# One level of Strassen's method in the up projection of a decoder step's MLP on one core

## What is computed

```python
def merge_and_mlp(x, o, pool_out, w_out, g_mlp, w_up, w_down):
    B, T, _ = x.shape
    mix = jnp.concatenate([o.reshape(B, T, ATTN_WIDTH).astype(x.dtype),
                           pool_out.astype(x.dtype)], axis=-1)
    h = x + mix @ w_out
    a = jnp.square(jax.nn.relu(rms_norm(h, g_mlp) @ w_up))
    return h + a @ w_down
```

## Time and profile before

| | |
|---|---|
| median of the runs | 899.13 us (897.83 to 900.75, 3 runs) |
| the profiled execution | 892.73 us, of which the trace spans 890.9 us |
| PE busy in the span | 819.0 us, 92% |
| DVE, ACT, POOL busy | 429.2 us, 345.5 us, 139.4 us |
| mean granted TensorE clock | 0.968 of 2.4 GHz |
| the MLP from the last W_out unit to the end | 464 us to 891 us of the span |

### The profile page before, as it was taken

One profiled execution on the slowest core, in us unless ns is written; L12 is line 12 of the kernel. 1 busy time (PEld: TensorE's weight loads), 2 busy tenths in 40 slices (PEclk: granted clock), 3 DMA queues, 4 the chain that ended last, 5 costly groups with the idle time before them and its releaser, 6 DMA issues.

```text
span 890.9 us, 18225 instructions
## 1 busy us (share of the span) xinstructions
PE 819.0 (92%) x7776; PEld 747.1 (84%) x7776; DVE 429.2 (48%) x800; ACT 345.5 (39%) x643; POOL 139.4 (16%) x166
## 2 busy tenths in 40 slices
PE   5999999997888867777999999999999999999997
PEld 4999987775555644557999999999999999999996
DVE  5434646664655476675237342334233433244554
ACT  6511155553466564563235331133212331033432
POOL 0001101100685336620220000000000000000122
PEclk8999999998899988999999999999999999999998
DMA  8922628852461115524522112222221122222222
GB/s 304 313 88 96 194 55 251 256 194 96 120 209 53 36 49 197 209 95 113 173 95 94 49 48 93 94 94 94 94 89 36 64 94 94 95 95 94 96 95 107
DMA packets 51946, 107.22 MB, mean 120 GB/s; under 512 B 7579, under 2 KB 21295, under 8 KB 49582
## 3 DMA queue, kind: packets, MB, share of 16 engines
q1 hardware_dynamic: 44973, 72.80, 24.7%
...
...
## 4 chain that ended last, share of the span: by engine, by line
PE 55%; POOL 2%; DMA 2%; issue 2%; DVE 2%; ACT 1%; SPq 0%; DVEq 0%; ACTq 0%; POOLq 0%
PE banks L1856 45%; PE banks L2147 5%; DMA low<-in_w_out 1%; PE banks L1668 1%; POOL zone L1439 1%; DMA low<-in_cache_slc,idx_slc 1%; DMA zone<-in_cache_slc,idx_slc 1%; PE banks L1736 1%; POOL zone L349 1%; POOL low L349 1%; PE banks L2157 0%; POOL rowsT L1439 0%; PE banks L1709 0%; PE banks L1687 0%; ACT xh L1862 0%
## 5 line engine op out<-in xcount | busy, mean ns | idle before, releaser
L1856 PE MATMUL banks<-xh,wh 128*128 128x288 f32 x640 | 137.9, 297 | 5.0 <-DVE wl L1841 2.5
L1856 PE MATMUL banks<-xl,wh 128*128 128x288 f32 x640 | 137.6, 297 | 0.0
L1856 PE MATMUL banks<-xh,wl 128*128 128x288 f32 x640 | 137.5, 296 | 0.0
L1836 ACT ACTIVATE wh<-low 128x1024 fp32r<-128x1024 f32 x79 | 82.4, 1050 | 112.7 <-PE banks L1856 102.8
L1856 PEld LDWEIGHTS banks<-xh,wh 128*128 128x128 f32 x640 | 103.4, 189 | 6.0 <-issue 3.2
L1856 PEld LDWEIGHTS banks<-xl,wh 128*128 128x128 f32 x640 | 103.7, 190 | 0.0
L1856 PEld LDWEIGHTS banks<-xh,wl 128*128 128x128 f32 x640 | 103.6, 190 | 0.0
L1841 DVE TENSOR_TENSOR wl<-low,wh 128x1024 fp32r<-128x1024 f32 x80 | 97.1, 1215 | 4.6 <-ACT wh L1836 4.6
L1856 PE MATMUL banks<-al,wh 128*128 128x288 f32 x384 | 82.3, 296 | 0.0
L1856 PE MATMUL banks<-ah,wl 128*128 128x288 f32 x384 | 82.3, 296 | 0.0
L1856 PE MATMUL banks<-ah,wh 128*128 128x288 f32 x384 | 82.2, 296 | 0.0
(11 more groups left out here) (349 smaller groups left out, 1563.0 us busy)
## 6 DMA issues: line engine op xcount, KB each, us to landing
...
```

The costliest lines, as they stand in the source:

```text
L1836: act.activation(wcols(m.wh, i), raw_cols(i), ACT.Copy).then_inc(wh_ready, 1)
L1856: last = pe.matmul(out(i, hf), w[wi], half(x[:, k, :], hf), start=first and part == 0, stop=end and part == 2)
```

## The change

The up projection is done two units at a time (a pair: 256 output features). The pair's weights, the features of x and the tokens are each cut in two halves, and the eight block products of 4 feature blocks x 288 tokens become seven by Strassen's method (J = 7): each is a product of a sum of weight blocks with a sum of x blocks. A block product is 4 x 3 = 12 matmuls, so a pair has 84 matmuls where two units had 96. The seven go to three PSUM banks (BANK); DVE and ACT read partial sums out while the bank is still being added to, and form the four outputs (even and odd unit, two halves) with the copies c1, u2 and u3. What is new around them:

- x: DVE, ACT and POOL form the seven x operands (m.xs, m.xt) of 128 x 1152 and split each in high and low, once, in the hinge. The gain is now applied by DVE for the first four blocks and by ACT for the others.
- weights: POOL forms four sums of 128 x 512 (`sums`) for each of the 16 pairs, and `hi` and `lo` split the seven weight operands of 128 x 512.
- taking out: per pair one ACT copy, five DVE additions and four DVE relus, each of 288 elements, in place of four relus of 288.
- loads: SP loads tiles of 256 columns (1 MB) for up and down, 36 in place of 18. A tile is asked for when the low parts of the tile two before are done.
- the weights of down units, the squaring and everything behind them are as before, at other places in the order.

The core of the diff:

```diff
+    J = 7
+    PER_Q, PAIRS = 36, 4
+    SUM_OF = {4: 0, 1: 1, 3: 2, 6: 3}
+    BANK = (0, 1, 0, 1, 2, 1, 2)
+    temps = [m.first_m[:, HALF * e:HALF * e + HALF] for e in range(4)]
...
+    def hi(act, q, p, j, first=False):
+
+        act.wait_ge(unit_mm, q * PER_Q + (5 + j // 2 if p == 0 else FIRST + J * (p - 1) + j + 1))
+        if j in SUM_OF:
+            act.wait_ge(s_ready, q * 16 + (4 * p + SUM_OF[j] + 1 + 2 * (not first)))
+        else:
+            act.wait_ge(sems.ring_in[p % 2], loaded_tile(q, p))
+        act.activation(m.wop_h[j], operand(p, j), ACT.Copy, scale=-1.0 if j == 5 else 1.0).then_inc(wh_ready, 1)
...
+        for t in range(8 * NQ + 4):
+            q, at = (t // 8, t % 8) if t < 8 * NQ else (NQ - 1, t - 8 * (NQ - 1))
+            sp.wait_ge(wl_ready, end(t - 2) if t >= 2 else 4)
+            if t < 2:
+                sp.wait_ge(sems.ring_in[t], W0)
+            if at < PAIRS:
+                src = m.w_up[0][:, 1024 * q + 256 * at:1024 * q + 256 * at + 256]
+            else:
+                d = (at - PAIRS) % 4
+                src = m.w_down[0][1024 * q:1024 * q + 1024, 256 * d:256 * d + 256]
+            sp.dma_start(m.raw_p[t % 2], src.rearrange("(k p) n -> p k n", p=P)).then_inc(sems.ring_in[t % 2], 16)
...
+            if 0 in part:
+                pool.wait_ge(sems.ring_in[p % 2], loaded_tile(q, p))
+                free(4)
+                pool.tensor_tensor(s1, a21, a22, ALU.add).then_inc(s_ready, 1)
+                pool.wait_ge(s_ready, done + 1)
+                pool.tensor_tensor(s2, s1, a11, ALU.subtract).then_inc(s_ready, 1)
+                pool.tensor_tensor(s3, a11, a21, ALU.subtract).then_inc(s_ready, 1)
+            if 1 not in part:
+                return
+            free(6)
+            if t == 0:
+                pool.wait_ge(wl_ready, FIRST)
+            pool.wait_ge(s_ready, done + 2)
+            pool.tensor_tensor(s4, a12, s2, ALU.subtract).then_inc(s_ready, 1)
...
+        hi(act, 0, 0, 4, True)
+        act.activation(m.xop_h[4], m.xt[:, 0], ACT.Copy).then_inc(xh_ready, 1)
+        hi(act, 0, 0, 5, True)
+        act.wait_ge(s_ready, T4)
+        act.activation(m.xop_h[5], m.xt[:, 3], ACT.Copy).then_inc(xh_ready, 1)
+        act.activation(m.xop_h[6], m.xs[:, 3], ACT.Copy).then_inc(xh_ready, 1)
...
+        def up(q, p):
+            if p == 0:
+                hi(act, q, 0, 6)
+            else:
+                activate(q, 2 * p - 2)
+            act.wait_ge(unit_mm, q * PER_Q + (FIRST + J * p + 1))
+            if p >= 2:
+                act.wait_ge(kept, q * UQ + (FIRST + 2 * p - 2))
+            act.activation(temps[p % 2], pb[3 * (p % 2)][:, 0:HALF], ACT.Copy).then_inc(c_kept, 1)
+            if p:
+                activate(q, 2 * p - 1)
+            if p < PAIRS - 1:
+                for j in range(J):
+                    hi(act, q, p + 1, j)
+            else:
+                for i in range(3):
...
-        for n in range(FIRST):
-            dve.wait_ge(xh_ready, KT_D + n + 1)
-            dve.scalar_tensor_tensor(out=m.xl[:, n, :], in0=m.hT[:, n, :], scalar=g_mlp[:, n:n + 1],
-                                     in1=m.xh[:, n, :].bitcast(F32), op0=ALU.mult, op1=ALU.subtract)\
+            if n == 6:
+                lo(dve, 0, 0, 0)
+        gains = lambda h: g_mlp[:, 4 * h:4 * h + 4].unsqueeze(2).broadcast_to([P, 4, HALF])
+        dve.wait_ge(kept, FIRST)
+        for e in range(2):
+            dve.tensor_tensor(m.xs[:, e], m.hT[:, 0:4, HALF * e:HALF * e + HALF], gains(0), ALU.mult)\
                .then_inc(xl_ready, 1)
+        dve.wait_ge(xl_ready, XS1)
+        dve.tensor_tensor(m.xt[:, 0], m.xs[:, 1], m.xs[:, 0], ALU.subtract).then_inc(xl_ready, 1)
+
+        def low_x(j, x):
+            dve.wait_ge(xh_ready, XHI[j])
+            dve.tensor_tensor(m.xop_l[j], x, m.xop_h[j].bitcast(F32), ALU.subtract).then_inc(xl_ready, 1)
+
+        dve.wait_ge(xl_ready, T1)
+        dve.wait_ge(xh_ready, XS22)
+        dve.tensor_tensor(m.xt[:, 1], m.xs[:, 3], m.xt[:, 0], ALU.subtract).then_inc(xl_ready, 1)
+        low_x(0, m.xs[:, 0])
+        lo(dve, 0, 0, 1)
+        dve.wait_ge(xl_ready, T2)
+        low_x(1, m.xt[:, 1])
+        lo(dve, 0, 0, 2)
+        low_x(2, m.xs[:, 2])
         dve.wait_ge(ssq_mm, 1)
         for hf in range(2):
             last = dve.tensor_scalar(half(m.var, hf), pb[6 + hf][:, 0:HALF], 1.0 / D, EPS, ALU.mult, ALU.add)
         last.then_inc(var_ready, 1)
+        lo(dve, 0, 0, 3)
+        low_x(3, m.xt[:, 2])
         dve.wait_ge(std_ready, 1)
         dve.reciprocal(m.rb, m.rb).then_inc(rb_ready, 1)
+        lo(dve, 0, 0, 4)
+        low_x(4, m.xt[:, 0])
+        lo(dve, 0, 0, 5)
+        low_x(5, m.xt[:, 3])
+        low_x(6, m.xs[:, 3])
...
+            if p:
+                low_act(q, 2 * p - 2)
+                low_act(q, 2 * p - 1)
+            ready(1)
+            dve.wait_ge(c_kept, q * PAIRS + (p + 1))
+            dve.tensor_tensor(u2, bank[1], c1, ALU.add).then_inc(u_read, 1)
+            if p == 0:
+                lo(dve, q, 0, 6)
+            ahead(0)
+            ready(2)
+            relu(half(odd, 0), bank[0], rb0)
+            ahead(1)
+            ready(3)
+            dve.tensor_tensor(u3, bank[1], c1, ALU.add).then_inc(u_read, 1)
+            ahead(2)
+            ready(4)
+            dve.wait_ge(u_read, q * 20 + (5 * p + 2))
+            dve.tensor_tensor(half(even, 1), bank[2], u3, ALU.add).then_inc(u_read, 1)
+            dve.wait_ge(u_read, q * 20 + (5 * p + 3))
+            relu(half(even, 1), half(even, 1), rb1)
+            ahead(3)
+            if p == PAIRS - 1:
+                down_low(dve, q, 0)
+            ready(5)
+            dve.tensor_tensor(half(even, 0), bank[1], c1, ALU.add).then_inc(u_read, 1)
+            dve.wait_ge(u_read, q * 20 + (5 * p + 4))
+            relu(half(even, 0), half(even, 0), rb0).then_inc(kept, 1)
+            ahead(4, 5)
+            if p == PAIRS - 1:
+                down_low(dve, q, 1)
+            ready(6)
+            dve.tensor_tensor(half(odd, 1), bank[2], u2, ALU.add).then_inc(u_read, 1)
+            dve.wait_ge(u_read, q * 20 + (5 * p + 5))
+            relu(half(odd, 1), half(odd, 1), rb1).then_inc(kept, 1)
+            ahead(6)
...
@@ -2119,23 +2357,45 @@
             last = pe.matmul(pb[6 + hf][:, 0:HALF], m.ones[:, :], half(m.sq[(KT_D - 1) % 2], hf), start=False,
                              stop=True)
         last.then_inc(ssq_mm, 1)
-        def unit(q, s, r, down, first_use, between=None):
-            n = q * UQ + s * 4 + (FIRST + 8 * down + r)
-            pe.wait_ge(wl_ready, n + 1)
-            pe.wait_ge(kept, n - 1)
+        def up(q, p, first=False):
+            s = 3 * (p % 2)
+            if p:
+                pe.wait_ge(kept, q * UQ + (FIRST + 2 * p - 2))
+            else:
+                pe.wait_ge(kept, q * UQ + (FIRST - 1))
+            for j in range(J):
+                pe.wait_ge(wl_ready, q * PER_Q + (FIRST + J * p + j + 1))
+                if first:
+                    pe.wait_ge(xl_ready, XLO + j)
+                if j == 2:
+                    pe.wait_ge(c_kept, q * PAIRS + (p + 1))
+                if j == 3:
+                    pe.wait_ge(u_read, q * 20 + (5 * p + 1))
+                if j == 4 and p == 0:
+                    pe.wait_ge(kept, q * UQ + FIRST)
+                if j == 5:
+                    pe.wait_ge(u_read, q * 20 + (5 * p + 2))
+                if j == 6:
+                    pe.wait_ge(u_read, q * 20 + (5 * p + 3))
+                for k in range(4):
+                    for part, (w, x) in enumerate(((m.wop_h, m.xop_h), (m.wop_h, m.xop_l), (m.wop_l, m.xop_h))):
+                        last = pe.matmul(pb[s + BANK[j]][:, 0:HALF], w[j][:, k, :], x[j][:, k, :],
+                                         start=j in (0, 1, 4) and k == 0 and part == 0, stop=k == 3 and part == 2,
+                                         skip_group_check=True)
+                last.then_inc(unit_mm, 1)
```

More of the change, by code:

```diff
@@ L322, in place_mlp @@
     m.var, m.rb = m.mixT[:, 4, :], m.mixT[:, 5, :]
-    m.y = sb("y", first, [P, TILES, D])
+    m.y = sb("y", first + 1024, [P, TILES, D])
+    spare, n = work + 5760, 4 * HALF
+    more = [m.low_at + 4096 + n * e for e in range(3)] + [spare, work + 9792, a["consts"] + P]
+    parts = [v.rearrange("p k t -> p (k t)")[:, n * e:n * e + n].rearrange("p (k t) -> p k t", k=4)
+             for v in (m.xh, m.xl) for e in range(4)]
+    parts += [sb(f"xop{e}", at, [P, 4, HALF], F32R)[:, :, :] for e, at in enumerate(more)]
+    m.xop_h, m.xop_l = parts[0:14:2], parts[1:14:2]
+    m.sums = [sb(f"wsum{e}", at, [P, 4, P])[:, :, :] for e, at in
+              enumerate((spare + n, a["consts"] + P + n, first + 1024, m.low_at + 4096 + 3 * n))]
+    m.xs, m.xt = sb("xs", zone, [P, 4, 4, HALF]), sb("xt", zone + 4 * n, [P, 4, 4, HALF])
+    blocks = [v for pair in zip(m.wh, m.wl) for v in pair][:7]
+    m.wop_h = [v[:, 0:512].rearrange("p (k n) -> p k n", k=4) for v in blocks]
```

(43 more changed lines are left out.)

182 lines of the change are left out of this document (114 added, 68 removed).

## The result

The changed kernel takes 941.53 us (median of 4 runs, 934.53 to 947.93) against 899.56 (4 runs, 897.83 to 900.75): a ratio of 1.047, 95% interval 1.039 to 1.054. It is 42 us slower; the forecast was 16, and the range ended at 931.

The account below looks back on a forecast made before the run. PE was taken to bound the kernel, by its matmul count times 0.1333 us plus its waits. Terms -25.6 + 22.8 + 15.5 + 1.1 + 1.7 + 0.3 = +15.8 us on 899.1 gave 915 us, range 892 to 931.

Parts of the forecast that it names:

- The matmuls: Up projection on PE: 192 matmuls of 288 columns removed at 0.1333 us each, -25.6 us.
- the hinge's order: Between last W_out result and up products: PE does three products, then waits for preparation; +16.9 us undisturbed, +22.8 with POOL.
- the places of the stalls: PE waits 1.95 us ahead of the fourth product in second and third pairs of each quarter, 8 in all, +15.5 us.
- I take 0.86, the row of the same size, and 1.10 as the upper bound: POOL's sum of 512 reads SBUF and holds up a DVE subtraction for 0.86 us, at most 1.10.
- the upper bound: Hinge and pairs with 1.10 us for each POOL sum: stalls of 2.9 us, total +28.4, 928 us.
- The rival without a delay: Hinge and pairs: a DVE subtraction is not delayed by a POOL addition; -3.3 us, 896 us; chance 0.26.
- The half clock as a rival of its own: Between pairs: each of 8 stalls brings half clock for 3.4 us, +13.6 us, 929 us; chance 0.09.
- Late tiles: Weight loads of 1 MB land in 12 us, POOL starts late, every pair loses another 1; 927 us; chance 0.05.
- The hinge as DVE's sum of work: Between W_out and up projection: DVE's work of 22.0 us plus 2.0 waiting for ACT sets the length, undisturbed.
- The rival of a hidden hinge: Preparation between W_out and up projection is hidden after all; 879 us; chance 0.04.

Follow-up runs that it names:

- a_cols4: Changed kernel with POOL's weight sums of every pair but the first formed for only 4 of 128 columns of each block; 900.8 us, 1.004 of the kernel before.
- c_fill: Changed kernel with 20 extra unread matmuls on PE ahead of the u2 wait in second and third pairs; 931.8 us, 1.039 of the kernel before.
- b_cols64: Changed kernel with POOL's weight sums of every pair but the first formed for 64 of 128 columns of each block; 907.1 us, 1.011 of the kernel before.
- d_u2first: Changed kernel with DVE's u2 placed ahead of the two low parts of activations; 919.7 us, 1.025 of the kernel before.
- f_hinge_order: Changed kernel with c1, u2 and u3 earlier and root and reciprocal later in the hinge, no work added or removed; 943.0 us, 1.049 of the kernel before.
- h: g_early_x with the weight sums on DVE instead of POOL; 902.3 us, 1.003 of the kernel before.
- j: Against h: ACT scales all x blocks, POOL's first sums start earlier, reciprocal in halves, c1 between square and rounded copy; 895.9 us, 1.001 of the kernel before.
- k: Against j: ACT splits weights first, c1 and one addition stand further ahead in second and third pair; 888.2 us, 0.990 of the kernel before.
- g_early_x: f_hinge_order with the x operands made block by block inside the W_out units; 935.7 us, 1.044 of the kernel before.

## Why the prediction was wrong

- **The matmuls, the hinge's order, the places of the stalls**: right. PE waits where the prediction said, for the releasers that it named (xh, c1, u2), 7.1, 1.1, 6.7 and 5.2 us against 6.5, 2, 8 and 6. The fourth product starts 31.9 us after the last kept result against 30.0; DVE's 1152 take 1.35 as forecast. The sum had the first three products at 1.6 us each and they took 3.2 at the lower clock; that cost nothing, since the waits behind them ended with ACT and DVE.
- **"I take 0.86, the row of the same size, and 1.10 as the upper bound"**: this step failed. The row has a broadcast operand, the sums have none, and one alone takes 1.29 us in place of 1.06 (that the broadcast makes the difference is argued, not tried). One sum holds DVE up by 1.79 - 0.68 = 1.11 us, and one x sum by 3.66 - 1.35 = 2.31 us in place of 1.9. The prediction had this price, from the 576 and 256 of the earlier trace rows, and all that it worked out from it came: stalls of 2.9, 1.0 in three first pairs, 24.7 in the hinge. Mis-sized by 0.25 us a sum, it moved the total by 12.6, to 928, which still lies in the range. The estimate from the page "GPSIMD Engine Reference" of the Trainium skill, Performance versus the Vector engine, was 1.1 us for 512; the trace agrees (1.11). The rival without a delay is refuted by the same rows and by a_cols4.
- **The half clock as a rival of its own**: the second failure, and what put the time outside the range. It had a chance of 0.09 at stalls of 2 us, and was added to the forecast, never to the upper bound. At stalls of 2.9 us the clock fell behind four of eight in the profiled execution, for 7.2 us, and c_fill gives 7.0 of the trace and 9.7 of the median back. With both, the prediction's own figures give 928 + 13.6 = 942. That this is the measured median is luck in part: 13.6 is eight drops of 1.7, the trace has four of 1.5 to 2.6, and the stalls and first pairs cost 3.8 more than the upper bound had. The two rivals were not independent: the longer hold makes the longer stall, and between pairs the clock fell behind stalls of 2.9 us and behind none of 0.7 to 1.4 (b_cols64, d_u2first).
- **Late tiles**: 1 MB lands in 5.5 us, and no wait of PE between pairs ends with a transfer; nothing is lost.
- **The hinge as DVE's sum of work**: right. f_hinge_order changes its order and moves the wait to the second pair; a_cols4, with POOL silent between pairs, is still no gain. The rival of a hidden hinge is refuted for this order; h, j and k show that it can be hidden in part, up to the point where DVE and POOL fill the W_out units too.

Left open: why the clock fell behind four of the stalls and not behind the others, which are as long. Three of the four stand in the second pair of a quarter whose first pair had stalled for 1.0 us too, and f_hinge_order has its drops behind stalls of 2.9 to 3.0 us at the same four places; but g_early_x has them behind two of its seven, one of them in a third pair of the second quarter. The trace before has two such idle times, and the prediction used only one of them: an idle time of 2.00 us ahead of 417.66 with the lower clock behind it, and one of 2.14 just before, behind which the granted clock stayed at 1.00:

```profile
412.24 0.51 PE L1856 MATMUL banks<-xh,wh 128*128 128x288 f32 x2 [2.14 <-DVE xl L1848]
...
412.00:417.00 5.00, 3.42 (x24) 3.21 (x24) 2.71 (x5) 2.74 (x4) 0.00 (x0) 1.00 0.40 131
```

Open too is how far DVE's work in the first three pairs could still be cut.
